# Seven products instead of eight in ten down projections of a one-core decoder layer

## Chip, core and metric

One Trainium2 chip; the kernel runs on one of its cores. The metric is the device time of one execution in microseconds. Before the change the median of three runs is 2538.48 us (2538.07 to 2540.17).

## What is computed

One layer of a hybrid decoder for 512 prompt positions and 8 single sample positions, 520 tokens in all, in float32. A first half mixes tokens (stick-breaking attention over 8 heads, with 1024 cached positions for each sample, and a chunked gating MLP), projects the result and adds it to the residual `h`. Then, with D_MODEL = 2048, D_FF = 5632 and PLE_DIM = 256:

```
f = rmsnorm(h, g_ffn)
h = h + (silu(f @ w_gate) * (f @ w_up)) @ w_down
h = h + sigmoid(rmsnorm(h, g_ple) @ w_ple_gate) * (p @ w_ple_proj)
```

The change touches the second of these lines.

## The kernel before

All activations lie transposed: 128 features on the partitions, 520 tokens in the free dimension, so `h` is 16 tiles of 128x520. The tokens are taken in two halves of 260. Every product of float32 matrices is made of three matmuls on halves rounded to a shorter format: high weight times high activation, high times low, low times high. Each weight block therefore needs a high half `w_hi` (a rounding copy on ACT, called a high below) and a low half `w_lo` (raw minus high, a subtraction on DVE, a low). A job is one such pair of operations on 1024 columns, 8 blocks of 128x128. Raw weights come from DRAM by DMAs that SP issues, one unit of 2048 columns (1024 KB) each.

The feed-forward runs over D_FF in 11 chunks of 512 features. Four blocks of features make a chunk, and they are computed in pairs: two feature blocks by 520 tokens by 2048 inputs is a 2x2 by 2x2 block product, done by seven products instead of eight (Strassen's scheme in Winograd's form). So a chunk has four pairs of tiles, two for the gate and two for the up projection, in the order g0, u0, g1, u1. Each pair (`pair_of_tiles`) has seven products of 24 matmuls of 128x260 (`product`), seven operand pairs `ops` that were built once from `f` on DVE and ACT ahead of and during the first pair, and four sums of weights on DVE (`add_weights`, into `w_sum` and in place of one raw half). Between the products ACT copies partial results from PSUM (`copy_part`) and DVE joins them (`join`); at the end of a gate pair ACT applies SiLU into `yg`, and at the end of an up pair DVE multiplies, ACT rounds `yg` into `act_hi` and DVE subtracts into `act_lo`.

The down projection of a chunk multiplies its 512 features by w_down into all 16 tiles of `h`. It is plain: `down_tiles` takes 16 tiles, for each 4 blocks x 3 terms x 2 token halves = 24 matmuls. ACT drains each finished tile from PSUM into one of four slots of `staging`, and POOL adds two slots at a time to the residual `h_dram` in DRAM by a DMA that accumulates (520 KB, `accum_op=ALU.add`). The down part of chunk c is placed behind the pair g0 of chunk c + 1, so there are ten such parts; the eleventh (`last_down`) adds straight into `h` in SBUF, reloaded from `h_dram`, and is followed by the gate of the last line of the reference, 16 tiles of 96 matmuls.

The order on every engine is written out by hand, and semaphores with counted values tie them together: `ended` counts products or tiles that PE has finished, `hi_done` and `lo_done` the jobs of ACT and DVE, `staged` the drains, `h_added` the landings of the accumulating DMAs, `w_summed` the sums of weights, `joined`, `copied`, `gate_read`, `up_read` and `silu_done` the steps at a pair's end. ACT, DVE and SP run the chunks 1 to 10 in a hardware loop (`Fori`), PE and POOL have them written out. The ring of `w_hi` and `w_lo` holds four jobs, the ring of raw weights three units (two in `w_raw`, one in `w_extra`). ACT makes the high half of the job four ahead of the product that just ended. SP's queue in the feed-forward holds only these loads, each behind a wait for a low or a sum that frees its slot, and at the end the reload of `h` in four DMAs of 1040 KB, and of `proj`.

Lines of the profile that are spoken of: L1737 mixer and output projection; L1954 plain matmuls (`plain_block`: down parts, last down part, gate, side projection); L1969 matmuls of pairs; L1041 highs; L1522 lows (L1260 those of the first half of the layer); L1535 sums; L1562 joins; L1126 drains; L1074 copied partial results; L795 accumulating DMAs; L739 loads of cached values; L790 the side projection's stores; L1615, L1620, L1627 operands of the first pair.

Of the kernel before, what the change touches and what calls it, by code (L numbers as in the profile page):

```python
# [27 lines left out]
P = 128  # L28
# [40 lines left out]
PAIR = 7  # L69
CHUNK_JOBS = 4 * PAIR + 2 * FFN_GROUP  # L70
CHUNK_ENDS = 4 * PAIR + KT
CHUNK_LOADS = 3 * FFN_GROUP
RAW_SLOTS = 3
JOB0 = 2 * U_FFN
STAGES = 4


Pair = namedtuple("Pair", "job end pair load")
Down = namedtuple("Down", "job end load")

PROJ_JOBS = 4
FIRST = [Pair(PROJ_JOBS + PAIR * i, KT + PAIR * i, i, 2 + 2 * i) for i in range(4)]


def chunk(job, end, pair, load):

    jobs, ends, loads = (PAIR, 2 * FFN_GROUP, PAIR, PAIR, PAIR), (PAIR, KT, PAIR, PAIR, PAIR), (2, 4, 2, 2, 2)
    out = []
    for i in range(5):
        if i == 1:  # L90
            out.append(Down(job, end, load))
        else:
            out.append(Pair(job, end, pair, load))
            pair += 1
        job, end, load = job + jobs[i], end + ends[i], load + loads[i]
    return out


LOOP = chunk(PROJ_JOBS + 4 * PAIR, KT + 4 * PAIR, 4, 2 + 8)
NEXT = chunk(LOOP[0].job + CHUNK_JOBS, LOOP[0].end + CHUNK_ENDS, 8, LOOP[0].load + CHUNK_LOADS)[0]  # L100
LAST_IT = FFN_CHUNKS - 2
LAST_DOWN = Down(NEXT.job + CHUNK_JOBS * LAST_IT, NEXT.end + CHUNK_ENDS * LAST_IT,
                 NEXT.load + CHUNK_LOADS * LAST_IT)
GATE_JOB = LAST_DOWN.job + 2 * FFN_GROUP
GATE_END = LAST_DOWN.end + KT
GATE_LOAD = LAST_DOWN.load + FFN_GROUP
# [84 lines left out]
def build(nc, w_units, x_t, p_t, cache_k, cache_v, page_table, g_mix, g_out, g_ffn, g_ple, g_q, g_k,  # L191
          ln_g, ln_b, w_s_t, b_s, sb_bias, w_s00, y_t, k_t, v_t, chunk_v_t):
    h_dram = nc.dram_tensor("h_dram", (P, KT, TOK), F32, kind="Internal").ap()
    proj_dram = nc.dram_tensor("proj_dram", (P, KT, TOK), F32, kind="Internal").ap()
    q_rows_dram = nc.dram_tensor("q_rows_dram", (SAMPLES, HEADS * P), F32, kind="Internal").ap()

    with ExitStack() as ctx:
# [18 lines left out]
        w_raw = sb("w_raw", [P, 2, SLOTS * P])  # L216
        w_hi = sb("w_hi", [P, 2, SLOTS * P], F32R)
# [33 lines left out]
        with ExitStack() as ffn:  # L251
            ops[6] = operand(6, ffn)
            act_hi = sb("act_hi", [P, FFN_GROUP, TOK], F32R, where=ffn)
            act_lo = sb("act_lo", [P, FFN_GROUP, TOK], F32R, where=ffn)
# [41 lines left out]
        with ExitStack() as ffn:  # L296
            staging = sb("staging", [P, STAGES, TOK], where=ffn)
            yg = sb("yg", [P, 2, TOK], where=ffn)
            part = sb("part", [P, 4, HALF], where=ffn)
            w_sum = sb("w_sum", [P, GROUPS * P], where=ffn)  # L300
            w_extra = sb("w_extra", [P, SLOTS * P], where=ffn)
# [16 lines left out]
        tok_ps = ctx.enter_context(nc.psum_tensor("tok_ps", [P, 512], F32))  # L318
        mix_ps = ctx.enter_context(nc.psum_tensor("mix_ps", [P, 512], F32))
# [14 lines left out]

        def raw(i):

            return w_extra[:, :] if i % RAW_SLOTS == 2 else w_raw[:, i % RAW_SLOTS, :]

        def landed(i, it=0):

            slot = i % RAW_SLOTS
            before = 0 if slot == 2 else U_FFN // 2
            return w_in[slot], 16 * (before + i // RAW_SLOTS + 1) + it * (16 * CHUNK_LOADS // RAW_SLOTS)

        def half_slot(w, job):

            return w[:, job % 4 // 2, job % 2 * GROUPS * P:(job % 2 + 1) * GROUPS * P]
# [10 lines left out]
        up_acc = (mix_ps[:, 0:HALF], out_ps[:, 1, 0:HALF], out_ps[:, 0, 0:HALF])  # L358
        pair = pair_ps[:, :, 0:HALF]
# [8 lines left out]
        w_in = [sem(f"w_in{i}") for i in range(RAW_SLOTS)]  # L368
# [12 lines left out]
        h_added = [sem(f"h_added{i}") for i in range(STAGES // 2)]  # L381
# [28 lines left out]
        act_hi_done = sem("act_hi_done")  # L410

# [72 lines left out]
        def _(sp):  # L484
# [52 lines left out]
            for u in range(U_FFN):  # L537
# [36 lines left out]
                if u == U_OUT_SB + 4:  # L574
                    sp.wait_ge(p_lo_done, 2)
                    sp.dma_start(raw(2), w_units[U_FFN]).then_inc(w_in[2], 16)
# [9 lines left out]
            def after_low(job, it=0):  # L586

                sp.wait_ge(lo_done, it * CHUNK_JOBS + (JOB0 + job + 1 - POOL_LO))

            def after_sums(pair, it=0):  # L590

                sp.wait_ge(w_summed, it * 16 + 4 * (pair + 1))

            def load(i, unit, it=0):

                if isinstance(it, int):
                    src = w_units[unit + it * CHUNK_UNITS]
                else:
                    src = w_units[bass.ds(it * CHUNK_UNITS + unit, 1), :, :].rearrange("a p n -> (a p) n")
                sp.dma_start(raw(i), src).then_inc(w_in[i % RAW_SLOTS], 16)  # L600

            after_low(1)
            load(3, U_FFN + 2)
            for k in range(KT - 2, KT):
                keep_h(k)
            after_low(3)
            load(4, U_FFN + 1)
            after_sums(0)
            load(5, U_FFN + 3)
            after_low(FIRST[0].job + 6)  # L610
            load(6, U_FFN + 4)
# [190 lines left out]
        def _(act):  # L802
# [408 lines left out]
            with act.Fori(0, LAST_IT) as it:  # L1211
                chunk_of_tiles(NEXT, it)
# [944 lines left out]
```

## Time and profile before

| | us |
|---|---|
| median of three runs | 2538.48 |
| the profiled execution | 2537.53 |
| its span | 2535.8 |
| PE busy, matmuls | 2492.0 |
| DVE busy | 1452.1 |
| ACT busy | 1014.6 |
| POOL busy | 235.1 |

The span is the time from the first to the last instruction that the profile holds; the execution's own time is 1.7 us more. Matmuls are pipelined: one is shown 282 ns long, but the next begins before it ends, so the pace is read from the length of a stretch and the number of matmuls in it. A row of a table by stage names the stretch in us from the span's start, its length, the busy time of each engine with the number of instructions, the granted TensorE clock as a share of full speed, the share of time in which the DMA engines were busy, and GB/s.

### The profile page before, as it was taken

How to read it: one execution, taken by the hardware profiler on the slowest of the kernel's cores; microseconds unless marked ns; L12 is line 12 of the kernel's file. 1: busy time of each engine (PE TensorE's matmuls, PEld its weight loads, DVE VectorE, ACT ScalarE, POOL GpSimd, SP SyncE). 2: the span in 40 equal slices, each digit the busy share in tenths (PEclk: the TensorE clock that was granted, in tenths of full speed). 3: DMA queues.
4: the chain of work that ended last, by engine and by line, in shares of the span. 5: the costliest groups of instructions: out<-in, count | busy, mean ns of one | idle time of the engine just before them, and what ended most of it. 6: DMA issues, size and time to landing. Idle time of an engine off the chain costs nothing.

```text
span 2535.8 us, 47986 instructions
## 1 busy us (share of the span) xinstructions
PE 2492.0 (98%) x20428; PEld 2469.4 (97%) x20428; DVE 1452.1 (57%) x1588; ACT 1014.6 (40%) x1351; POOL 235.1 (9%) x266
## 2 busy tenths in 40 slices
PE   6998999999999998999999999999999999999999
PEld 6998999999999998999999999999999999999999
DVE  6368776554446468555555555555555555557433
ACT  4333233333433364444444444444444444445221
POOL 4000111011101220000000000000000000003000
PEclk9999999999999999999999999999999999999999
DMA  4245665554432442454545454545444554445322
GB/s 184 101 159 191 242 217 215 184 192 142 161 116 101 159 152 100 138 130 140 128 141 126 142 126 142 126 142 126 142 126 142 126 143 125 143 125 201 137 98 85
DMA packets 73343, 368.58 MB, mean 145 GB/s; under 512 B 9658, under 2 KB 9658, under 8 KB 45378
## 3 DMA queue, kind: packets, MB, share of 16 engines
q1 hardware_dynamic: 50994, 285.29, 31.7%
q0 software_dynamic: 22016, 80.42, 15.0%
q8 instruction: 161, 2.64, 0.4%
q14 instruction: 28, 0.23, 0.0%
q10 hardware_dynamic: 144, 0.01, 0.0%
HBM read 305.98 MB, written 59.70 MB: 144 GB/s over the span
## 4 chain that ended last, share of the span: by engine, by line
PE 92%; DVE 6%; DMA 1%; issue 1%; ACT 0%; SPq 0%; DVEq 0%; ACTq 0%
PE out_ps L1954 27%; PE out_ps L1737 22%; PE pair_ps L1969 12%; PE mix_ps L1969 10%; PE out_ps L1969 7%; PE tok_ps L1969 5%; PE out_ps L1859 4%; PE pair_ps L1776 1%; DVE x_lo L1269 1%; DVE w_lo L1260 1%; DVE op_lo L1627 1%; DVE dot_s L1292 1%; DVE k_ring L1291 1%; PE tok_ps L1844 0%; DMA k_ring<-cache_k 0%
## 5 line engine op out<-in xcount | busy, mean ns | idle before, releaser
L1737 PE MATMUL out_ps<-x_hi,w_hi 128*128 128x260 f32 x1792 | 382.1, 295 | 20.3 <-DVE w_lo L1260 10.5
L1522 DVE TENSOR_TENSOR w_lo<-w_raw,w_hi 128x1024 fp32r<-128x1024 f32 x196 | 238.9, 1223 | 234.7 <-ACT w_hi L1041 234.7
L1737 PE MATMUL out_ps<-x_hi,w_lo 128*128 128x260 f32 x1792 | 363.7, 285 | 0.0
L1737 PE MATMUL out_ps<-x_lo,w_hi 128*128 128x260 f32 x1792 | 363.0, 284 | 0.0
L1737 PEld LDWEIGHTS out_ps<-x_hi,w_hi 128*128 128x128 f32 x1792 | 281.2, 191 | 24.8 <-DVE w_lo L1260 9.4
L1954 PE MATMUL out_ps<-act_hi,w_hi 128*128 128x260 f32 x1400 | 281.7, 282 | 0.0
L1954 PE MATMUL out_ps<-act_lo,w_hi 128*128 128x260 f32 x1400 | 280.8, 282 | 0.0
L1954 PE MATMUL out_ps<-act_hi,w_lo 128*128 128x260 f32 x1400 | 280.3, 281 | 0.0
L1737 PEld LDWEIGHTS out_ps<-x_hi,w_lo 128*128 128x128 f32 x1792 | 279.1, 190 | 0.0
L1737 PEld LDWEIGHTS out_ps<-x_lo,w_hi 128*128 128x128 f32 x1792 | 278.8, 190 | 0.0
L1041 ACT ACTIVATE w_hi<-w_raw 128x1024 fp32r<-128x1024 f32 x196 | 205.4, 1052 | 141.7 <-PE out_ps L1954 75.5
L1969 PE MATMUL pair_ps<-op_hi,w_hi 128*128 128x260 f32 x880 | 249.7, 284 | 6.7 <-issue 3.4
L1969 PE MATMUL pair_ps<-op_hi,w_lo 128*128 128x260 f32 x880 | 250.2, 284 | 0.0
L1969 PE MATMUL pair_ps<-op_lo,w_hi 128*128 128x260 f32 x880 | 249.7, 284 | 0.0
L1522 DVE TENSOR_TENSOR w_lo<-w_sum,w_hi 128x1024 fp32r<-128x1024 f32 x132 | 161.7, 1225 | 134.6 <-ACT w_hi L1041 133.4
L1954 PEld LDWEIGHTS out_ps<-act_lo,w_hi 128*128 128x128 f32 x1400 | 216.3, 188 | 0.0
L1954 PEld LDWEIGHTS out_ps<-act_hi,w_lo 128*128 128x128 f32 x1400 | 215.8, 188 | 0.0
L1954 PEld LDWEIGHTS out_ps<-act_hi,w_hi 128*128 128x128 f32 x1400 | 214.9, 188 | 0.0
L1126 ACT ACTIVATE staging<-out_ps 128x520 f32<-128x520 f32 x160 | 97.1, 607 | 285.0 <-PE out_ps L1954 285.0
L814 ACT ACTIVATE w_hi<-w_raw 128x1024 fp32r<-128x1024 f32 x116 | 116.4, 1050 | 220.6 <-PE out_ps L1737 219.6
L1969 PE MATMUL mix_ps<-op_hi,w_hi 128*128 128x260 f32 x704 | 198.7, 282 | 2.7 <-ACT part L1074 2.6
L1522 DVE TENSOR_TENSOR w_lo<-w_extra,w_hi 128x1024 fp32r<-128x1024 f32 x100 | 121.9, 1223 | 137.6 <-ACT w_hi L1041 137.6
(247 smaller groups left out, 5505.9 us busy)
## 6 DMA issues: line engine op xcount, KB each, us to landing
w_raw<-w_units SPq DMA_DIRECT2D x155, 1024.0 KB, 4.8
w_extra<-w_units SPq DMA_DIRECT2D x50, 1024.0 KB, 4.8
h_dram<-staging POOLq DMA_DIRECT2D x80, 520.0 KB, 5.6
k_ring<-cache_k SPq DMA_DIRECT2D x50, 512.0 KB, 5.1
v_ring<-cache_v POOLq DMA_DIRECT2D x43, 512.0 KB, 4.9
acc<-cache_v POOLq DMA_DIRECT2D x21, 512.0 KB, 4.8
k_third<-cache_k SPq DMA_DIRECT2D x14, 512.0 KB, 4.4
h<-x_t SPq DMA_DIRECT2D x4, 1040.0 KB, 10.5
```

The lines of the kernel that those rows point to most:

```text
L814: act.activation(w_hi[:, u % 2, cols], w_raw[:, u % 2, cols], ACT.Copy).then_inc(hi_done, 1)
L1041: act.activation(half_slot(w_hi, job), src, ACT.Copy).then_inc(hi_done, 1)
L1126: act.activation(halves(staging[:, t % STAGES, :]), tile_ps(t), ACT.Copy).then_inc(staged, 1)
L1260: dve.tensor_tensor(w_lo[:, u % 2, cols], w_raw[:, u % 2, cols], w_hi[:, u % 2, cols], ALU.subtract).then_inc(lo_done, 1)
L1269: dve.scalar_tensor_tensor(out=x_lo[:, slot, :], in0=src, scalar=gain, in1=x_hi[:, slot, :], op0=ALU.mult, op1=ALU.subtract).then_inc(x_lo ...
L1291: chained(dve.tensor_tensor(k_slot(j), k_slot(j), q_rows[:, :], ALU.mult))
L1292: dve.tensor_reduce(dot_s[:, pg * HEADS:(pg + 1) * HEADS], k_slot(j).rearrange("p (h d) -> p h d", h=HEADS), AXIS.X, ALU.add)\
L1522: dve.tensor_tensor(half_slot(w_lo, job), src, half_slot(w_hi, job), ALU.subtract)\
L1737: mm = pe.matmul(out_ps[:, 2 * (t % 2) + a, 0:HALF], w[:, u % 2, cols], x[:, a * HALF:(a + 1) * HALF], start=first and n == 0, stop=last a ...
L1859: mm = pe.matmul(o_s_ps(u)[:, hd:hd + 1], v_slot(j)[:, hd * P:(hd + 1) * P], a_s[:, b % 3, at:at + 1], start=False, stop=j == pages[-1], s ...
L1954: mm = pe.matmul(tile[:, a, :], w, x[:, a * HALF:(a + 1) * HALF], start=first and n == 0, stop=last and n == 2)
L1969: mm = pe.matmul(acc, w, x[:, g, :], start=fresh and g == 0 and n == 0, stop=g == GROUPS - 1 and n == 2, skip_group_check=True)
```

## The change

The ten down parts are computed by the same scheme of seven products. A unit of w_down (512 features by 4 tiles of outputs) is taken as 2x2 blocks of 256 by 256, the chunk's activations as 2x2 blocks of 256 features by 260 tokens. There are four units in a part, so 28 products, each of 2 x 2 blocks x 3 terms = 12 matmuls of 128x260, into 2x260 columns of PSUM. Products 3, 4 and 6 of a unit run on top of products 0, 1 and 2 in the same banks, so some of the final additions happen there; those that remain go through DRAM.

- ACT drains each of the 28 products as 2x260 columns, into six slots (four of `staging`, two made of `part`), product k behind the landing of product k - 6.
- POOL issues 28 accumulating DMAs of 260 KB a part instead of 8 of 520 KB. Four of seven add one quarter (two tiles by half the tokens, so two pieces of 1040 bytes in each partition) to `h_dram`; three go to helper arrays `q_dram`, `r11_dram`, `r22_dram` (2080 bytes in one piece), which the first part writes and the others add to. After the tenth part five accumulating DMAs inside DRAM add the helper arrays to `h_dram`, and SP waits for them before it reloads `h`.
- DVE makes four sums of 512 columns for each unit; highs and lows in a down part are 28 of 512 columns instead of 8 of 1024. The operands `b11`, `b2`, `t13`, `t24` are built from `yg` in the following gate pair: four differences and four lows on DVE, four highs on ACT. The eleventh part keeps `act_hi` and `act_lo`.
- The ring of `w_hi` and `w_lo` is six pieces of 512 columns, three jobs of a pair; the room of the fourth holds `w_sum` and a fifth slot of raw weights. Raw weights lie in five slots of 1024 columns and are loaded by halves of a unit, 512 KB each.
- The feed-forward of SP, ACT and DVE is written out, with no hardware loop, from a plan made when the program is built (`ITEMS`, `HIGHS`, `FREED`, `LOADS`). In the first pair one subtraction of the side projection's weights is placed before the last tile of the output projection, and the order of sums, lows and highs is changed.

```diff
 def add_job(size, end):
+    pos = JOB_POS[-1] + JOB_SIZE[-1] if job else 0
+    for i in range(pos, pos + size):
+        HOLDER[i] = job
+    FREED.append(JOB_END[HOLDER[pos + size - 1 - SUBS]] if job >= PROJ_JOBS - 1 else 0)
...
+DOWN_BANKS = (bank_x, bank_z, bank_v, bank_x, bank_z, bank_y, bank_v)
+DOWN_BEFORE = (None, None, None, 0, 1, None, 2)
...
 # PE
-def down_tiles(item, free, it=0):
-    for t in range(KT):
-        if t % 2 == 0:
-            after_low(item.job + t // 2, it)
-        free(t)
-        for k in range(FFN_GROUP):
-            plain_block(item.job + t // 2, t % 2 * FFN_GROUP + k, tile_ps(t), act_hi[:, k, :],
-                        act_lo[:, k, :], k == 0, k == FFN_GROUP - 1)
+def down_tiles(item):
+    pair0 = 4 * (item.n + 1)
+    pe.wait_ge(act_lo_done, lows_of_up(2 * (item.n + 1)))
+    for k in range(DOWN_JOBS):
+        u, i = divmod(k, UNIT_JOBS)
+        job = item.jobs + k
+        if k == 1:
+            pe.wait_ge(joined, 3 * pair0)
+        elif k == 2:
+            pe.wait_ge(gate_read, 2 * (item.n + 1) + 1)
+            pe.wait_ge(joined, 3 * pair0 + 1)
+        elif k == 5:
+            pe.wait_ge(joined, 3 * pair0 + 3)
+            pe.wait_ge(up_read, 2 * (item.n + 1))
+        before = [j for j in range(k) if DOWN_BANKS[j % UNIT_JOBS] is DOWN_BANKS[i]]
+        if before:
+            pe.wait_ge(staged, DOWN_JOBS * item.n + before[-1] + 1)
+        after_low(job)
+        fresh = DOWN_BEFORE[i] is None
+        for a in range(2):
+            for c in range(2):
...
+                for n, (w, x) in enumerate(((w_h, hi), (w_h, lo), (w_l, hi))):
+                    mm = pe.matmul(DOWN_BANKS[i][:, a, :], w, x, start=fresh and c == 0 and n == 0,
+                                   stop=c == 1 and n == 2, skip_group_check=True)
+        mm.then_inc(ended, 1)
...
 # ACT
+def high(job, dst, src):
+    act.wait_ge(ended, FREED[job])
+    act.activation(dst, src, ACT.Copy).then_inc(hi_done, 1)
+def down_tiles(item):
+    for k in range(DOWN_JOBS):
+        if k == STAGES:
+            act.wait_ge(joined, 3 * (4 * (item.n + 1) + 1))
+            act.wait_ge(silu_done, 2 * (item.n + 1) + 1)
+        if stage_uses(item.n, k):
+            act.wait_ge(h_added[k % DOWN_STAGES], 16 * stage_uses(item.n, k))
+        after_end(item.end + k + 1)
+        act.activation(stage(k), DOWN_BANKS[k % UNIT_JOBS], ACT.Copy).then_inc(staged, 1)
+        highs(item.end + k + 1)
...
 # POOL
-            pool.dma_start(h_dram[:, m:m + 2, :], staging[:, slot:slot + 2, :], accum_op=ALU.add)\
-                .then_inc(h_added[slot // 2], 16)
+for n in range(FFN_CHUNKS - 1):
+    extra = ALU.add if n else ALU.bypass
+    for k in range(DOWN_JOBS):
+        u, i = divmod(k, UNIT_JOBS)
+        pairs = slice(2 * u, 2 * u + 2)
+        dst, op = ((residual(u, 0, 0), ALU.add), (residual(u, 1, 1), ALU.add), (r22_dram[:, pairs, :], extra),
+                   (q_dram[:, pairs, :], extra), (residual(u, 0, 1), ALU.add),
+                   (r11_dram[:, pairs, :], extra), (residual(u, 1, 0), ALU.add))[i]
+        pool.wait_ge(staged, DOWN_JOBS * n + k + 1)
+        pool.dma_start(dst, stage(k), accum_op=op).then_inc(h_added[k % DOWN_STAGES], 16)
+for i in range(DOWN_STAGES):
+    pool.wait_ge(h_added[i], 16 * stage_uses(FFN_CHUNKS - 1, i))
+pool.dma_start(quarter(1, 1), sums_of(q_dram), accum_op=ALU.add).then_inc(merged[0], 16)
...
+pool.wait_ge(merged[0], 16 * 4)
+pool.dma_start(quarter(1, 1), sums_of(r22_dram), accum_op=ALU.add).then_inc(merged[1], 16)
...
 # DVE
+def down_sums(item, u, n):
+    h0, total = item.loads + 2 * u, as_blocks(down_sum(u))
+    if n == 0:
...
+        add_weights(total, blocks_of(h0 + 1, 0), blocks_of(h0 + 1, 1))
+        dve.wait_ge(w_summed, item.sums + 4 * u + 1)
+        add_weights(blocks_of(h0 + 1, 0), blocks_of(h0, 0), blocks_of(h0 + 1, 0), ALU.subtract)
+    elif n == 1:
+        after_low(item.jobs + UNIT_JOBS * u + 1)
+        add_weights(total, total, blocks_of(h0, 0), ALU.subtract)
+    else:
+        after_low(item.jobs + UNIT_JOBS * u + 3)
+        add_weights(total, blocks_of(h0, 1), total, ALU.subtract)
...
+def down_weights(item, after):
+    low_down(item, 6)
+    for u in range(1, 4):
+        down_sums(item, u, 0)
+        low_down(item, UNIT_JOBS * u)
+        low_down(item, UNIT_JOBS * u + 1)
+        down_sums(item, u, 1)
...
+        down_sums(item, u, 2)
+        for k in range(4, UNIT_JOBS):
+            low_down(item, UNIT_JOBS * u + k)
+    for stage in range(4):
+        begin(after, stage)
```

## Rows read from the trace of the kernel before

**Rows 1.** The page: busy time, and the chain that ended last, by engine.

```profile
PE 2492.0 (98%) x20428; PEld 2469.4 (97%) x20428; DVE 1452.1 (57%) x1588; ACT 1014.6 (40%) x1351; POOL 235.1 (9%) x266
...
PE 92%; DVE 6%; DMA 1%; issue 1%; ACT 0%; SPq 0%; DVEq 0%; ACTq 0%
```

**Rows 2.** Waits of PE from 890 us on: us in total, times, longest.

```profile
PE pair_ps L1969 <- issue: 3.4, 2, 2.0
PE pair_ps L1969 <- DVE w_lo L1522: 3.4, 1, 3.4
```

**Rows 3.** Table by stage: a down part, the four pairs beside it.

```profile
1055.90:1101.80 45.90, 45.90 (x387) 45.90 (x386) 13.29 (x11) 17.37 (x25) 6.04 (x7) 1.00 0.74 161
1101.80:1182.24 80.44, 80.44 (x674) 80.44 (x674) 58.13 (x61) 37.84 (x51) 0.85 (x1) 1.00 0.37 120
```

**Rows 4.** The chain in order of time: start, us, what.

```profile
922.20 1.14 DVE w_lo L1260
...
1055.92 45.87 PE out_ps L1954 x384
```

**Rows 5.** Timeline of DVE: start, us, what.

```profile
1037.29 0.42 DVE L1589 SCALAR_TENSOR_TENSOR yg<-mix_ps,yg 128x260 f32<-128x260 f32 x1
1037.63 0.42 DVE L1591 SCALAR_TENSOR_TENSOR yg<-part,yg 128x260 f32<-128x260 f32 x1
...
1093.08 1.22 DVE L1535 TENSOR_TENSOR w_extra<-w_raw,w_extra 128x1024 f32<-128x1024 f32 x1
1094.22 1.22 DVE L1535 TENSOR_TENSOR w_sum<-w_sum,w_raw 128x1024 f32<-128x1024 f32 x1
```

**Rows 6.** Timeline of ACT in a down part.

```profile
1061.69 0.61 ACT L1126 ACTIVATE staging<-out_ps 128x520 f32<-128x520 f32 x1 [2.26 <-PE out_ps L1954]
1062.19 1.05 ACT L1041 ACTIVATE w_hi<-w_extra 128x1024 fp32r<-128x1024 f32 x1
1064.56 0.61 ACT L1126 ACTIVATE staging<-out_ps 128x520 f32<-128x520 f32 x1 [1.31 <-PE out_ps L1954]
```

**Rows 7.** DMAs issued by POOL, by form: busy us, mean ns, idle before.

```profile
L795 POOL DMA_DIRECT2D h_dram<-staging x80 | 68.3, 854 | 1232.2 <-ACT staging L1126 1215.3 <-issue 16.9
L739 POOL DMA_DIRECT2D v_ring<-cache_v x43 | 23.5, 547 | 188.0 <-PE out_ps L1859 177.9 <-issue 10.1
...
L790 POOL DMA_DIRECT2D proj_dram<-proj_stage x16 | 8.7, 544 | 14.2 <-ACT proj_stage L1028 13.8 <-POOL h_sum L780 0.3
```

**Rows 8.** DMA, 1096.9 to 1102.7 us: busy tenths, GB/s, GpSimd's queue.

```profile
DMA  1010100000990434589599989899897712000000
GB/s 29 0 29 0 29 0 0 0 0 0 287 172 0 29 29 86 86 143 201 115 230 201 230 172 258 172 230 230 172 287 143 144 29 29 0 0 0 0 0 0
...
q0 software_dynamic: 148, 0.55, 59.5%
```

**Rows 9.** DMA, 1101.8 to 1182.24 us: the hardware queue.

```profile
q1 hardware_dynamic: 1225, 8.99, 32.1%
```

**Rows 10.** DMA, 1081.8 to 1092 us: two accumulating, one load of weights.

```profile
DMA  9469899999995779979699759989998963100000
GB/s 131 49 114 179 163 261 212 212 212 212 354 257 225 289 289 418 418 321 482 257 387 307 210 177 195 196 163 212 245 212 163 245 114 65 16 16 0 0 0 0
...
q0 software_dynamic: 269, 0.99, 55.2%
q1 hardware_dynamic: 144, 1.05, 28.5%
```

**Rows 11.** DMAs, KB, us to landing: page; last row 920.7 to 941 us.

```profile
h_dram<-staging POOLq DMA_DIRECT2D x80, 520.0 KB, 5.6
k_ring<-cache_k SPq DMA_DIRECT2D x50, 512.0 KB, 5.1
...
proj_dram<-proj_stage POOLq DMA_DIRECT2D x13, 260.0 KB, 3.5
```

**Rows 12.** Timeline of POOL: an issue that met a DVE operation.

```profile
1062.60 0.91 POOL L795 DMA_DIRECT2D h_dram<-staging  x1 [122.53 <-ACT staging L1126]
```

More of the change, by code:

```diff
@@ L68 @@
 GROUPS = KT // 2
[L69 to L73, printed above, removed]
+SUB = GROUPS * P // 2
+SUBS = 6
+RAW_SLOTS = 5
 JOB0 = 2 * U_FFN
 STAGES = 4
-Pair = namedtuple("Pair", "job end pair load")
-Down = namedtuple("Down", "job end load")
+DOWN_STAGES = 6
 PROJ_JOBS = 4
[L82 to L96, printed above, removed]
@@ L99 @@
[L99 to L106, printed above, removed]
+UNIT_JOBS = 7
+DOWN_JOBS = 4 * UNIT_JOBS
+Pair = namedtuple("Pair", "n end jobs loads sums downs")
@@ new lines, with add_job @@
+Down = namedtuple("Down", "n end jobs loads sums")
+Plain = namedtuple("Plain", "end jobs loads")
+Load = namedtuple("Load", "unit half slot turn after")
+JOB_POS, JOB_SIZE, JOB_END, FREED, LOADS = [], [], [], [], []
+HIGHS = defaultdict(list)
+HOLDER = {}
+FREE = deque([(0, "low", 0), (1, "low", 1), (2, "low", 2), (4, "out", U_OUT + 2 * KT), (3, "low", 3)])
+def add_job(size, end):
+    job = len(JOB_POS)
+    pos = JOB_POS[-1] + JOB_SIZE[-1] if job else 0
+    JOB_POS.append(pos)
+    JOB_SIZE.append(size)
+    JOB_END.append(end)
+    for i in range(pos, pos + size):
+        HOLDER[i] = job
+    FREED.append(JOB_END[HOLDER[pos + size - 1 - SUBS]] if job >= PROJ_JOBS - 1 else 0)
+    return job
@@ new lines, in add_down, with add_plain @@
+def add_down(n, end, sums, unit):
+    item = Down(n, end, len(JOB_POS), len(LOADS), sums)
+    for k in range(DOWN_JOBS):
+        HIGHS[FREED[add_job(1, end + k + 1)]].append((item, k))
+    for u in range(4):
+        for half in range(2):
+            add_load(unit + u, half)
+        for half in range(2):
+            release(item.loads + 2 * u + half, "low", item.jobs + UNIT_JOBS * u + 5 + half)
+    return item
+def add_plain(end, unit, units, ends):
+    item = Plain(end, len(JOB_POS), len(LOADS))
+    for k in range(2 * units):
+        HIGHS[FREED[add_job(2, end + ends(k))]].append((item, k))
+        add_load(unit + k // 2, k % 2)
+        release(item.loads + k, "low", item.jobs + k)
+    return item
@@ L602, in _ @@
[L602 to L611, printed above, removed]
-            after_sums(1)
-            load(7, U_FFN + 6)
-            after_low(FIRST[1].job + 6)
-            load(8, U_FFN + 5)
-            after_sums(2)
-            load(9, U_FFN + 7)
```

726 lines of the change are left out of this document (400 added, 326 removed).

## The prediction

> **What bounds the kernel now.** I read the page's busy shares and chain first. PE is busy 98% of the span and holds 92% of the chain [rows 1]. The list of who waited for whom, for PE from 890 us on, is nearly empty: 10.7 us in all, of which the two longest are in the first pair of tiles [rows 2]. From 1055.9 us the table by stage shows PE busy for the whole of each stretch at a granted clock of 1.00 [rows 3]: a down part takes 45.9 us for 384 matmuls (0.1195 us each), the four pairs beside it 80.4 us for 672 (0.1197 us). In the chain a down part is one unbroken PE piece [rows 4]. So in the feed-forward nothing but the number of matmuls counts, and every one taken away is worth 0.1195 us as long as no other engine, queue or transfer becomes slower than PE. Before that, in the first pair, the chain goes through DVE [rows 4].
>
> **What the change takes off PE.** A down part was 16 tiles x 4 blocks x 3 terms x 2 halves = 384 matmuls of 128x260. It becomes 4 units x 7 products x 4 blocks x 3 terms = 336 of the same shape, each with its own weight load as now. 48 x 0.1195 = 5.73 us a part, 57.3 us in ten. A product of a unit takes 12 x 0.1195 = 1.43 us, a part 28 x 1.43 = 40.1 us.
>
> **What DVE gets.** Two 1024-column operations start 1.14 us apart, two of 260 columns 0.34 us [rows 5]; by the line between them 512 columns cost 0.60 us. A unit needs four sums and seven subtractions of 512 columns, 11 x 0.60 = 6.6 us in its 10.0 us of PE. In a gate pair the building of the operands adds five operations of 260 columns and three of 520 (0.61 us): 3.5 us onto seven subtractions and four sums of 1.14 and three joins of 0.34, 17.1 us beside 20.1 us of PE; the subtraction of 1040 columns in each up pair goes. DVE stays below PE in both. Following the order written out, a low half in a down part is done some 1.9 us after the product six before it ended, and PE needs it 7.2 us after. With room for three jobs of 1024 columns instead of four, a pair's low half still has two products, 5.7 us, for a high half of 1.05, a low half of 1.22 and at most two sums. Zero; if this cover went, a late low half would cost PE its lateness once per product.
>
> **What ACT gets.** A drain of 520 columns and a high half of 512 start about 0.5 us apart each [rows 6]: 1.0 to 1.2 us per 1.43 us product. The tightest place is the start of a part: after the gate pair ends, ACT makes two high halves, the first behind a sum, then three SiLUs, and only then drains product 0, about 3.4 us after the pair's end, while PE wants that bank at 3 x 1.43 = 4.3 us, and the bank of the gate sum at 2.9 us against some 1.6. Both fit by 1 us. Zero, with 3 us a part as the other end (a rival).
>
> **What POOL and the DMA get.** Here the trace shows no like of what is added. Eight accumulating DMAs of 520 KB a part become 28 of 260 KB: 4.26 MB become 7.45 MB. Sixteen of them write two pieces of 1040 bytes a partition, twelve a whole 2080. POOL first. Issuing took 0.854 us for the accumulating 128 rows, 0.544 us for a plain 128 rows, whether of 2080 or of 4096 bytes [rows 7]; so it goes by rows and kind, not by bytes. For 256 pieces the nearest bounds are 0.85 (pieces free) and 1.71 us (twice). I take the upper end: 12 x 0.86 + 16 x 1.71 = 37.7 us in 40.1.
> Then the engines. In a stretch with one accumulating DMA alone, the digits of the busy row add up to 16.3 slices of 0.145 us, 2.36 us, and as digits are cut down, up to 2.6; take 2.5 us for 520 KB, 1.25 us for 260 KB, and this is what the 215 GB/s of its full slices gives too [rows 8]. The queue's own share counts overlapping packets twice and is the upper bound: 59.5% of 5.8 us = 3.45 us, 1.73 us for 260 KB. The lower bound is the plain rate, 0.7 us. Weights run at the same time: the hardware queue took 32.1% of 80.44 us for 8.99 MB [rows 9], so 1.50 us for a 512 KB half unit, eight in a part, 12.0 us. Together 28 x 1.25 + 12.0 = 47.0 us of work in a part of 40.1 us. Where both kinds ran together now, 0.99 and 1.05 MB were done in 7.2 us of busy engines (the digits give 26.8 slices of 0.255 us, 6.8 us, plus half of what they cut off) against 4.7 + 3.0 = 7.7 one after the other [rows 10], so about 45 us. Some of this may run late. Drain k waits only for the landing of k - 6, 6 x 1.43 - 0.6 = 8.0 us after it was staged; landing took 5.6 us for 520 KB [rows 11], so 4.3 to 5.2 us for 260 KB (half the movement, up to twice the issue), which leaves about 3.3 us; and PE returns to a bank after three products at the earliest, 2.3 us after a prompt drain, less what ACT is busy with, 1.7 us. Cover: 5 us a part. 45 - 5 = 40 to 47.0 - 5 = 42.0 us: a stall of 0 to 1.9 us a part. I take 1.0, so 10 us in ten, with 0 and 15.3 us a part (28 x 1.73 + 12.0 - 5 - 40.1) as ends.
> A rule of the Trainium skill speaks against such transfers: "DMA: Bandwidth & Descriptors", "Anatomy of one DMA", gives each one from GpSimd about 2.0 us and its bytes over 436 GB/s, an estimate of 2.6 us here and 73 us for 28 if nothing overlaps. The sum would then be about 2537.5 + 10 x (73 - 45.9) = 2809 us. The thirteen plain DMAs of 260 KB that landed 3.5 us after issue within 20.3 us [rows 11] overlap, so the fixed part is latency here; as a rival it has rival 5.
>
> **The rest.** Weight halves of 512 KB land in 5.1 us [rows 11]; in the order of loads the tightest one has 4.5 us before DVE's sum and that sum 3 us of its own. Zero. The first pair: one 1024-column subtraction moves ahead of DVE's chain into its idle time, -1.1 us [rows 4, 5]; the loads it needs are out before. The join at the end: five accumulating DMAs inside DRAM with 1024 pieces each, by 0.854 us per 128 about 6.8 us to issue, 34 us, plus two landings of some 8 us: 50 us in the 54.6 us between the tenth part's end and the moment SP loads the residual again. Zero, up to 10 us once if the pieces cost more. Loops written out on ACT, DVE and SP: PE shows no gap at them, zero. The last down part and the gate keep their matmuls; half the gate's weights of a tile can be prepared only one tile ahead, 5.7 us for about 3.7 us of work. Zero.
>
> **Sum.** From the profiled execution, 2537.5 us (its span of 2535.8 and 1.7 around it): -57.3 -1.1 +10 = 2489.1. The median of the runs is 1.0 us above the profiled one: 2490 us.
>
> **Rivals.**
> 1. The accumulating queue becomes the bound: slower. Place: drains on ACT waiting for landings, and PE waiting for drains, in the ten down parts. At 1.73 us a transfer a part takes 28 x 1.73 + 12.0 - 5 = 55.4 us against 45.9 before: +9.5 x 10, 2633 us. It decides from 1.38 us a transfer, where a part is as long as before. For it: 74% of the engines' time is busy in a down part already [rows 3], and both the bytes and the number of pieces grow. Against: the peaks of 290 GB/s for accumulation alone and over 450 GB/s with weights beside it [rows 8, 10]. 15%.
> 2. The same, only between: 1.32 to 1.38 us a transfer. At 1.35 a part takes 44.8 us, 4.7 us over PE: 2527 us. 12%.
> 3. POOL's issuing is the bound. It needs over 2.17 us for 256 pieces ((40.1 + 5 - 10.3)/16). If each of them also waited for one of DVE's 0.60 us operations, 1.71 + 0.60 = 2.31: a part of 42.3 us, +22, 2502 us. One issue that met a DVE operation took 0.91 instead of 0.85 us [rows 12], which speaks against it. 8%. The Trainium skill, "SBUF — State Buffer", "SBUF: two separate sides", says that DVE keeps GpSimd off a shared port pair in two-port modes, or with two SBUF sources if the GpSimd operation reads SBUF; the row agrees that writing descriptors beside such sums is hardly held up.
> 4. The change doesn't deliver its 5.7 us: ACT's queue at the start and end of each part is late by 3 us, 30 us in all, 2510 us. For it: the margins of 1 us above. Against: before, ACT idles more than a microsecond ahead of each drain [rows 6]. 10%.
>
> 5. The transfers don't overlap at all: a landing of 4.3 us each, 28 x 4.3 = 120 us a part, 3280 us. Against it the overlap in [rows 11]; 1%, and taken out of the 15% of rival 1. The rule of "DMA: Bandwidth & Descriptors" above is its milder form.
>
> **Chances and range.** The forecast (a stall of 0 to 2 us a part, 2479 to 2500) has 55%. Noise is about 0.2%, 5 us. Faster: 55 + 10 + 8 and most of the second rival, 80%; within 0.2%, 5%; slower, 15%. The range goes from 2476 (no stall at all and a better start) to 2540; what it leaves out is rival 1 and little else.
>
> **What would show it.** Down parts of 336 matmuls and 40 to 42 us, pairs still 80.4 us; DMA busy 0.9 or more in a down part; ACT's drains waiting for landings late in a part, by less than 1 us each. POOL issues of 1.7 us for the split rows and 0.86 for the others. It is wrong if parts are 45 us or longer (rivals 1 and 2: waits for landings; rival 3: POOL never idle in a part), if pairs grow beyond 81 us (the shorter rings), or if the last down part begins late behind the reload of the residual.

## The result and the profile after

The changed kernel takes 2572.65 us (median of 4 runs, 2568.15 to 2580.49) against 2538.28 us before (2537.31 to 2540.17). The ratio is 1.0138, 95% interval 1.0110 to 1.0166: it is slower by 1.4%, and the forecast of 2490 us and its range of 2476 to 2540 were wrong. The profiled execution took 2575.6 us (span 2574.0) beside 2537.5 before.

The page of the changed kernel: busy time, the accumulating queue, the chain by engine.

```profile
PE 2468.4 (96%) x19948; PEld 2439.2 (95%) x19948; DVE 1692.9 (66%) x2088; ACT 1170.9 (45%) x1731; POOL 473.3 (18%) x471
...
q0 software_dynamic: 75728, 117.71, 23.1%
...
PE 64%; DMA 16%; DVE 12%; ACT 4%; issue 3%; POOL 1%; SPq 0%; DVEq 0%; ACTq 0%; POOLq 0%
...
h_dram<-staging POOLq DMA_DIRECT2D x130, 260.0 KB, 9.8
```

The 480 matmuls are gone, but PE's share of the chain fell from 92% [rows 1] to 64%, and transfers hold 16%. A landing takes 9.8 us for 260 KB, where it took 5.6 us for 520 KB [rows 11]. The list of PE's waits, nearly empty in this part of the kernel before [rows 2], has three new entries (us in total, times, longest):

```profile
PE tok_mix L2118 <- ACT staging L1240: 27.5, 10, 4.1
PE pair_ps L2181 <- ACT staging L1240: 26.1, 19, 2.1
...
PE out_ps L2102 <- DVE h L1859: 8.4, 1, 8.4
```

And behind ACT's drains stand the landings; the list of waits of ACT:

```profile
ACT staging L1240 <- DMA h_dram<-staging: 96.1, 93, 3.7
```

L2181 is a product of a down part, L1240 its drain, L2118 a pair of tiles. In nearly every one of the ten parts PE waits twice for a bank whose drain waits for a slot of the ring, and once more, mostly longest, at the first product of the next pair. The table by stage shows one period: the pairs, the down part with its waits, and what follows.

```profile
1746.07:1829.90 83.83, 83.83 (x687) 83.83 (x688) 66.99 (x83) 40.26 (x60) 2.11 (x2) 0.98 0.41 118
1829.90:1875.81 45.91, 39.45 (x323) 38.86 (x322) 28.61 (x41) 30.66 (x55) 27.97 (x26) 1.00 1.08 225
1875.80:1881.00 5.20, 5.19 (x30) 5.20 (x31) 2.21 (x2) 2.01 (x4) 2.11 (x2) 0.67 1.16 215
```

The period is 129.7 us, from one such wait's end to the next, against 126.3 before [rows 3]. In the part's stretch 6.5 us are idle on PE, the DMA share is 1.08, and POOL, the engine that issues the 28 transfers, is busy for 28.0 of 45.9 us. A DMA share above 1 is possible because the view adds up packets that overlap. The third row is the surprise: behind the wait the granted clock is 0.67 over 5.2 us. PE's timeline shows it in the starts of its matmuls: 0.12 us apart at first, 0.22 us apart from 1876.77 to 1879.8, then 0.12 again.

```profile
1875.81 0.36 PE L2118 MATMUL tok_mix<-op_hi,w_hi 128*128 128x260 f32 x1 [3.44 <-ACT staging L1240]
...
1876.48 0.29 PE L2118 MATMUL tok_mix<-op_hi,w_lo 128*128 128x260 f32 x1
1876.60 0.37 PE L2118 MATMUL tok_mix<-op_hi,w_hi 128*128 128x260 f32 x1
1876.77 0.42 PE L2118 MATMUL tok_mix<-op_lo,w_hi 128*128 128x260 f32 x1
1876.99 0.42 PE L2118 MATMUL tok_mix<-op_hi,w_lo 128*128 128x260 f32 x1
...
1879.81 0.40 PE L2118 MATMUL tok_mix<-op_hi,w_hi 128*128 128x260 f32 x1
```

That is the lower level of 1.2 GHz for about 3 us. The product takes 4.63 us instead of 2.87, so the stall costs 1.76 us more than its own 3.4. The same happens at eight of the ten pair starts, and not only behind the long waits. Two of the starts with a short wait, from the timeline, and their products, from the chain:

```profile
1746.07 0.36 PE L2118 MATMUL tok_mix<-op_hi,w_hi 128*128 128x260 f32 x1 [1.91 <-ACT staging L1240]
2265.87 0.36 PE L2118 MATMUL tok_mix<-op_hi,w_hi 128*128 128x260 f32 x1 [1.87 <-ACT staging L1240]
```

```profile
1746.07 4.65 PE tok_mix L2118 x24
2265.87 3.13 PE tok_mix L2118 x24
```

The first of them is slow, the second isn't. In the three parts that end with such a short wait, 24 matmuls behind the wait before it, inside the part, were slow too (4.2 to 4.5 us instead of 3.0, behind waits of 1.72, 1.75 and 2.13 us), while other waits of 1.71 and 1.74 us had no such effect. So the length of one wait alone doesn't tell whether the clock falls.

The chain of waits goes along the ring (start, us, what):

```profile
1841.66 10.48 DMA h_dram<-staging
1852.14 0.02 issue
1852.16 0.61 ACT staging L1240
1852.77 0.29 issue
1853.06 1.20 POOL h_dram L870
1854.26 0.16 issue
1854.42 9.78 DMA h_dram<-staging
...
1865.13 9.78 DMA h_dram<-staging
1874.90 0.02 issue
1874.92 0.61 ACT staging L1240
1875.54 0.28 issue
1875.81 4.63 PE tok_mix L2118 x24
```

A slot comes round in 10.7 us (1854.42 to 1865.13), about 9.8 of them a landing. Six slots give one transfer per 1.785 us, and a product takes 1.43 us. The DMA view of this stretch (busy tenths, GB/s, queues):

```profile
DMA  0289599999999999999999999999999999999999
GB/s 14 43 246 198 90 262 250 187 212 204 193 197 224 335 316 322 241 200 198 205 203 195 205 222 308 322 324 259 208 191 204 197 198 202 247 327 320 326 216 194
...
q0 software_dynamic: 5034, 6.07, 82.3%
q1 hardware_dynamic: 1152, 4.19, 25.8%
```

From the sixth slice on the engines are full. The movement is near 200 GB/s where accumulation is alone and 310 to 330 where a weight load runs beside it. Between 1850 and 1856 us almost nothing but accumulation runs; the queue's line for these 6 us, and the one for the whole period from 1746.07 to 1875.81 us:

```profile
q0 software_dynamic: 938, 1.20, 118.6%
```

```profile
q0 software_dynamic: 6092, 7.47, 35.4%
```

So 260 KB take 1.33 us of full engines (1.20 MB in 6 us, 200 GB/s). By the queue's share, which counts overlapping packets twice and therefore passes 100%, it is 0.354 x 129.74 / 28 = 1.64 us each. The stretch of the part alone can't be divided by 28: only 6.07 MB, 22.8 transfers' worth, moved in it, and the last ones land behind it.

### The profile page after: what moved, and what is told of

Read it like the earlier page. It is cut to its first block, busy times and chain, and to the rows that moved or that the text cites. A ratio compares the mean times of both kernels' runs of the same rounds, so it can differ in the third digit from the quotient of the medians.

```text
span 2574.0 us, 47687 instructions
## 1 busy us (share of the span) xinstructions
PE 2468.4 (96%) x19948; PEld 2439.2 (95%) x19948; DVE 1692.9 (66%) x2088; ACT 1170.9 (45%) x1731; POOL 473.3 (18%) x471
## 3 DMA queue, kind: packets, MB, share of 16 engines
q0 software_dynamic: 75728, 117.71, 23.1%
## 4 chain that ended last, share of the span: by engine, by line
PE 64%; DMA 16%; DVE 12%; ACT 4%; issue 3%; POOL 1%; SPq 0%; DVEq 0%; ACTq 0%; POOLq 0%
PE out_ps L1885 22%; DMA h_dram<-staging 14%; PE tok_mix L2118 12%; PE out_ps L2102 9%; PE pair_ps L2118 7%; PE out_ps L2118 6%; PE out_ps L2007 4%; DVE w_lo L1613 3%; DVE w_sum L1625 2%; ACT w_hi L1132 1%; ACT staging L1240 1%; PE pair_ps L1924 1%; POOL h_dram L870 1%; DMA k_ring<-cache_k 1%; DVE x_lo L1358 1%
## 5 line engine op out<-in xcount | busy, mean ns | idle before, releaser
L1613 DVE TENSOR_TENSOR w_lo<-w_sum,w_hi 128x1024 fp32r<-128x1024 f32 (+1 forms) x252 | 244.7, 971 | 179.1 <-ACT w_hi L1132 176.7
L1132 ACT ACTIVATE w_hi<-w_raw 128x1024 fp32r<-128x1024 f32 (+1 forms) x306 | 264.2, 866 | 159.2 <-PE out_ps L2102 103.1
L2118 PE MATMUL tok_mix<-op_hi,w_hi 128*128 128x260 f32 x1056 | 303.7, 288 | 29.0 <-ACT staging L1240 27.5
L1132 ACT ACTIVATE w_hi<-w_sum 128x1024 fp32r<-128x1024 f32 (+1 forms) x252 | 214.8, 852 | 204.4 <-DVE w_sum L1625 152.2
L2118 PE MATMUL tok_mix<-op_hi,w_lo 128*128 128x260 f32 x1056 | 304.0, 288 | 0.0
L2118 PE MATMUL tok_mix<-op_lo,w_hi 128*128 128x260 f32 x1056 | 303.2, 287 | 0.0
L2118 PE MATMUL pair_ps<-op_hi,w_hi 128*128 128x260 f32 x880 | 249.5, 283 | 8.7 <-DVE op_lo L1793 5.0
L2118 PE MATMUL pair_ps<-op_hi,w_lo 128*128 128x260 f32 x880 | 249.8, 284 | 0.0
L2118 PE MATMUL pair_ps<-op_lo,w_hi 128*128 128x260 f32 x880 | 249.4, 283 | 0.0
L2118 PEld LDWEIGHTS tok_mix<-op_hi,w_hi 128*128 128x128 f32 x1056 | 204.4, 194 | 31.0 <-issue 29.3
L905 ACT ACTIVATE w_hi<-w_raw 128x1024 fp32r<-128x1024 f32 x115 | 115.3, 1049 | 221.4 <-PE out_ps L1885 220.3
L2118 PEld LDWEIGHTS tok_mix<-op_hi,w_lo 128*128 128x128 f32 x1056 | 204.3, 194 | 0.0
L2118 PEld LDWEIGHTS tok_mix<-op_lo,w_hi 128*128 128x128 f32 x1056 | 204.2, 193 | 0.0
L2118 PEld LDWEIGHTS pair_ps<-op_hi,w_hi 128*128 128x128 f32 x880 | 166.8, 190 | 9.4 <-issue 7.5
```

Source lines behind the costliest of these rows:

```text
L905: act.activation(w_hi[:, u % 2, cols], w_raw[:, u % 2, cols], ACT.Copy).then_inc(hi_done, 1)
L1132: act.activation(dst, src, ACT.Copy).then_inc(hi_done, 1)
L1613: dve.tensor_tensor(slot(w_lo, job), src, slot(w_hi, job), ALU.subtract).then_inc(lo_done, 1)
L2118: mm = pe.matmul(acc, w, x[:, g, :], start=fresh and g == 0 and n == 0, stop=g == GROUPS - 1 and n == 2, skip_group_check=True)
```

## Experiments

Each ratio is against runs of the kernel before taken beside it: 2537.12 us for e1, e2, e3 and e5, 2537.64 us for e4, e6, e7 and e8, 2537.37 us for e9, e10 and e11.

**e1: the same transfers, nothing added.**

```diff
-                    pool.dma_start(dst, stage(k), accum_op=op).then_inc(...)
+                    pool.dma_start(dst, stage(k), accum_op=ALU.bypass).then_inc(...)
```

> The changed kernel with all 28 DMAs of a down part as plain writes, so the residual and the helper arrays hold only the last part's products: the addition is left out, all else stays. Theory (the accumulating transfers fill the DMA engines in the down parts, some 1.33 us for 260 KB, and ACT's drains wait for landings): a plain 260 KB takes 0.7 us, 28 x 0.7 + 12 = 32 us of work in 41 us, so the 6.4 us of waits and the 1.6 us of low clock behind them go from each part: about 2495 us, 8 us of which are the late weights at the end. Rival (POOL's issuing or ACT's order are what is late): no more than 10 us better, about 2562. Rival (PE's own pace in the down part is the loss, 0.1226 us a matmul): parts without waits and the pace stays, which would leave 10 us of the loss.

Measured: 2494.44 us, ratio 0.9831 (0.9814 to 0.9847). The page, and behind it two rows of the chain, the starts of a pair five periods apart:

```profile
q0 software_dynamic: 38096, 117.71, 13.7%
...
h_dram<-staging POOLq DMA_DIRECT2D x130, 260.0 KB, 4.7
```

```profile
1580.14 2.88 PE tok_mix L2118 x24
```

```profile
2185.81 2.88 PE tok_mix L2118 x24
```

From 1190 to 2150 us PE waits for nothing. The queue moves the same bytes and lands in 4.7 us instead of 9.8. The period is (2185.81 - 1580.14) / 5 = 121.1 us. So 78 us of the changed kernel's time are the price of adding instead of writing. This also measures the gain by itself: 5.2 us a period, not 5.7. The total met the expected 2495 us partly by luck: 8 us of it were to come from the late weights at the end, and PE still waits there for 6.8 us instead of 8.4.

**e3: the kernel before, its accumulating transfers issued twice.**

```diff
+                    pool.dma_start(spare_dram[:, m:m + 2, :], staging[:, slot:slot + 2, :],
+                                   accum_op=ALU.add).then_inc(h_added[slot // 2], 16)
```

> The kernel before (plain down parts, 384 matmuls) with each accumulating DMA of 520 KB issued twice, the second into a spare array: 8.5 MB a part in pieces as before. Theory (bytes of accumulation fill the engines at about 200 GB/s beside the weights): 16 x 2.6 + 12 = 54 us of work in a part of 45.9 us with two pairs of slots to run late: parts of 48 to 52 us, 2560 to 2600 us, without any product of the new scheme. Rival (it is the latency of each transfer against a ring of six slots of 1.43 us): here a slot has 11.5 us for two transfers of 5.6 us, no wait: 2538 to 2542 us.

Measured: 2590.63 us, ratio 1.0205 (1.0188 to 1.0222), as expected: such traffic alone, with no Strassen product in a down part, slows the kernel before too. The waits count both landings. ACT's longest wait in the down parts is for them:

```profile
ACT staging L1129 <- DMA spare_dram<-staging: 202.5, 53, 6.6
```

**e2: no 1040-byte pieces.** The residual in DRAM is laid out by quarters, so that each transfer writes whole 2080-byte rows.

```diff
-    h_dram = nc.dram_tensor("h_dram", (P, KT, TOK), ...)
+    h_dram = nc.dram_tensor("h_dram", (P, 4, 2, 2, 2, HALF), ...)
```

> The changed kernel with the residual kept in DRAM as quarters (two tiles by half the tokens in one row of 2080 bytes a partition), so no transfer of a down part has pieces of 1040 bytes; the stores and the reload of the residual carry the pieces instead. Theory (bytes fill the engines): POOL's issues fall from 1.2 to 0.9 us, the rate stays near 200 GB/s, less than 3 us a part: 2545 to 2572 us. Rival (the pieces are what is slow): the 16 split transfers of a part lose 0.2 us or more each, the waits of 6.4 us a part go below 3 and the clock stays up: 2520 us or less.

Measured: 2556.34 us, ratio 1.0069 (1.0050 to 1.0088), inside the theory's window and far above the rival's 2520. The issue of a split transfer falls from 1.24 to 0.87 us and the landing from 9.8 to 9.0: 16 us less than the changed kernel, a fifth of the 78. The stores and the reload of `h` change with the layout (16 loads of 260 KB for four of 1040); PE's wait at the last down part stays near what it was, 7.8 us.

**e5: each down part cut into two halves**, with a pair of tiles between them, so that 14 transfers come at a time.

```diff
-            if c and i == 0:
-                items.append(add_down(c - 1, end, sums, unit + 8))
...
+            if c and i < 2:
+                items.append(add_down(c - 1, end, sums, unit + 8 + 2 * i, PART_JOBS * i))
...
```

> The changed kernel with each down part cut in two: units 0 and 1 behind the first gate pair of the next chunk, units 2 and 3 behind its first up pair, so a pair of 20 us lies between them; same matmuls, transfers, sums. Theory (the engines' throughput over a part of 41 us is what is short): 14 x 1.33 + 6 = 25 us of work in 20.5 us, of which 5 us may run late, and the pair behind it takes up the rest: waits below 1 us a half, no low clock: about 2495 us. Rival (latency of a transfer against the ring of six slots): the waits come from the seventh drain on in each half, 8 of 14 drains a half wait: 2540 us or more.

Measured: 2597.77 us, ratio 1.0246 (1.0229 to 1.0263). My theory was wrong here: this is slower than the changed kernel. PE's waits:

```profile
PE tok_mix L2146 <- ACT staging L1258: 32.2, 15, 3.5
PE out_ps L2130 <- DVE h L1887: 22.9, 2, 12.3
```

The chain shows landings of 9.5 to 10.7 us in these short halves too, and the pair behind a first half still waits 2.9 to 3.5 us for the last drains, with the lower clock behind it. So it isn't the mean load of the period that counts, but the rate inside a burst: a ring of six slots fills within six products. But the cut isn't a clean test of that. Waits for drains fell from 53.6 to 34.1 us in all, and some 20 us of new waits for copied partial results and low halves took their place, so that a period is 129.7 us as in the changed kernel. The 25 us by which this kernel is slower come for the most part from the end: in the chain the merge's landings (27.9 and 9.6 us) now stand ahead of the reload, the waits at the last down part are 22.9 us instead of 8.4, and the granted clock is 0.93 from 2250 to 2450 us.

**e4: proj's load moved behind four weight loads** at the last down part.

```diff
-            sp.dma_start(proj[:, 0:HEADS, :], ...)
             for i in range(LAST_DOWN.loads + 3, GATE.loads + 2 * KT):
                 load(i)
+                if i == LAST_DOWN.loads + 6:
+                    sp.dma_start(proj[:, 0:HEADS, :], ...)
```

> The changed kernel with one load moved: the 2 MB of proj that the first gate needs goes out behind the first four weight halves of the gate's ring instead of ahead of them. Theory (at the last down part the raw weights stand behind the reload of h and proj, and PE waits 8.4 us once for an h add that waits for a split): about 8 us less than the changed kernel, 2562 to 2567. Rival (the h adds wait for the reload of h itself, the weights are hidden): 2570 to 2575, no change.

Measured: 2567.84 us (2562.58 to 2569.92), ratio 1.0113 (1.0097 to 1.0130). It is 4.8 us less than the changed kernel, between the windows of theory and rival; but the ranges of the two kernels overlap, and of the 6.6 us between their profiled executions 5.1 are there by some 920 us, ahead of everything that the edit touches. What the traces show is the wait for the h add: it falls from 8.4 to 4.7 us, so the order of the loads is some half of that wait.

**e6: five slots instead of six.**

```diff
-DOWN_STAGES = 6
+DOWN_STAGES = 5
```

> The changed kernel with five staging slots instead of six for the down parts. Theory A (the part is bound by how many bytes a microsecond the DMA engines get through with accumulating writes and weights together; six slots only stand in a queue, 10.7 us a slot's cycle is six times 1.785): fewer slots in flight, each lands sooner, time unchanged, 2570 to 2580. Theory B (each accumulating transfer has a latency of about 9.8 us that doesn't depend on what else is in flight, and the ring is too short for it): the cycle stays 10.7 us, 2.14 us a transfer instead of 1.785, +0.355 x 28 = 10 us a part, 2660 to 2680. In between (latency partly queueing): about 2600.

Measured: 2606.34 us, ratio 1.0265 (1.0248 to 1.0283), +34 us, the case in between. The median landing falls from 9.8 to 8.0 us, which is close to what a queue with five instead of six in it would give, and yet the kernel is slower. Lower clock is part of it: the first product of a pair takes up to 5.5 us instead of 4.6. So a landing is for a good part queueing behind the other slots, and a latency remains that five slots cover less well; how the 34 us divide isn't shown, and no run has more than six slots. ACT's waits for it (96.1 us in the changed kernel):

```profile
ACT staging L1240 <- DMA h_dram<-staging: 153.0, 111, 4.5
```

**e8: half of each addition left out.**

```diff
+                    tiles = slice(0, 2 if op is ALU.bypass else 1)
-                    pool.dma_start(dst, stage(k), accum_op=op).then_inc(...)
+                    pool.dma_start(dst[:, tiles, :], stage(k)[:, tiles, :], accum_op=op).then_inc(...)
```

> The changed kernel with every accumulating transfer cut to its first tile (130 KB instead of 260 KB); the second tile isn't added. Number of transfers, waits and slots as they are. Theory A (bytes set the time of accumulation): 28 x 0.68 + 12 = 31 us in a part of 40, no waits for staging, 2495 to 2502. Rival (a fixed time per transfer, or the issue on POOL, sets it): 2555 to 2575.

Measured: 2492.29 us, ratio 0.9829 (0.9811 to 0.9846), 3 us below theory A's window and far from the rival's. With the number of transfers and the waits kept, half the bytes land in 5.8 us and all the waits for drains in the parts go. So the number of transfers doesn't set the price. The pieces of a split transfer are halved with the bytes (128 instead of 256, issued in 0.87 instead of 1.24 us), so this run alone doesn't tell bytes from pieces; e2, with the bytes kept and the pieces halved, gained 16 of the 78 us, which leaves most to the bytes that are added.

**e7: helper arrays written plainly, added later.** In eight of ten parts the twelve transfers to the helper arrays write fresh arrays. Twelve accumulations inside DRAM add them during the next pairs, whose DMA share is 0.41. It has e2's layout and e4's order too.

```diff
+                late = 0 < n < FFN_CHUNKS - 2
+                to_q, to_r11, to_r22 = (q_new, r11_new, r22_new) if late else (q_dram, r11_dram, r22_dram)
...
+                    for total, new in ((r22_dram, r22_new), (q_dram, q_new), (r11_dram, r11_new)):
+                        for i in range(0, HEADS, 2):
+                            pool.dma_start(total[:, i:i + 2, :], new[:, i:i + 2, :], accum_op=ALU.add).then_inc(...)
```

> h kept in DRAM by quarters (no 1040-byte pieces), proj's load moved as in the tail run, and in eight of the ten down parts the twelve transfers to the helper arrays are plain writes into fresh arrays, which are added to the running ones by twelve DRAM to DRAM accumulations during the next pairs of tiles. Theory (only accumulating transfers inside the down part are too dear; 16 x 1.36 + 12 x about 0.5 + 12 of weights = 40 us in a part of 40 us; the pairs' 80 us have room for 12 accumulations): the waits for staging nearly vanish in eight parts, 2490 to 2505, below both kernels. Rival (the accumulations disturb the pairs' weights, or the remaining sixteen still land in over 8 us): 2520 to 2550.

Measured: 2507.88 us (2497.80 to 2509.88), ratio 0.9871 (0.9847 to 0.9896), 3 us over the theory's window and below both kernels. PE's waits for drains, 53.6 us together in the changed kernel, are now

```profile
PE pair_ps L2196 <- ACT staging L1255: 3.5, 4, 1.3
PE tok_mix L2133 <- ACT staging L1255: 3.4, 2, 2.8
```

of which 5.0 us are in the tenth part, which isn't deferred. That part shows the old picture, the clock included:

```profile
2198.00:2204.00 6.00, 3.21 (x23) 3.04 (x22) 3.50 (x3) 3.18 (x5) 2.19 (x4) 0.89 1.11 262
2204.00:2210.00 6.00, 6.00 (x44) 6.00 (x44) 3.11 (x3) 2.37 (x5) 0.68 (x1) 0.83 1.09 243
```

**e11: the same kernel once more.**

> The deferred kernel once more, unchanged, for a narrower interval: 2500 to 2510.

Measured: 2507.81 us, ratio 0.9886 (0.9871 to 0.9900). This is the version to keep: 1.1% to 1.3% below the kernel before, 2.5% below the changed one.

**e9: the deferral alone**, on the changed kernel.

> The changed kernel with one thing altered: in eight of the ten down parts the twelve helper transfers are plain writes into fresh arrays, added to the running ones during the next pairs of tiles. h stays in its old layout (1040-byte pieces), proj's load where it was. Theory (sixteen accumulations instead of twenty-eight in a part are what counts, the layout was worth 16 us only because the ring was full): 2505 to 2525. Rival (the small pieces cost the same 1.6 us a part whatever else is in flight): 2507.88 + 16 + 5 = 2529 or more.

Measured: 2526.24 us (2517.76 to 2530.16), ratio 0.9950 (0.9935 to 0.9964), 1 us over the theory's window. Deferral takes 46 us off the changed kernel by itself. The time lies between the windows of theory and rival (2525 and 2529), and the runs scatter more than that, so it doesn't decide what the pieces cost when the ring is less full. The remaining 18 us to e7 are near the 16 and 5 that layout and load order were worth with a full ring. In the traces PE waits 18.9 us for drains here and 7.4 in e7, and 7.9 and 2.7 us at the last down part, together 16.7 of the 18.

**e10: e7 with the later additions left out.**

> The deferred kernel without the twelve DRAM to DRAM accumulations during the pairs: the fresh arrays are written and never added. Theory (plain writes in the part are nearly free, the accumulations in the pairs delay some weights by a few us in all): 2495 to 2503. Rival (they cost nothing, what is left of the distance to the run without any addition, 2494.44, is in the parts): 2505 to 2510.

Measured: 2501.44 us (2494.04 to 2503.42), ratio 0.9863 (0.9848 to 0.9877). About 6 us are the price of the additions beside the pairs, as the theory had it: e11, taken beside it, is 6.4 us slower and the two ranges don't meet, though e7's overlaps this one.

## Why the prediction was wrong, step by step

**PE.** The mechanism was right, the size a little off: -5.2 us a part by e1's period, -52 us instead of -57.3. In e1 a product of a down part takes 1.44 to 1.46 us instead of 1.43, without any wait; 28 of them are about 0.5 us. Why isn't settled.

**First pair.** From the output projection's last matmul to the first down part it was 143.2 us before, 140.7 to 140.8 in the changed kernel, e1 and e8, 142.4 in e4: -0.8 to -2.5 us instead of -1.1.

**DVE and ACT.** Zero was right: with plain writes (e1) PE waits for neither from 1190 to 2150 us, so the margin of 1 us held and rival 4 falls.

**POOL.** A split row's transfer was issued in 1.2 us, not 1.71, a whole one in 0.9 to 1.0. POOL idles 18 us in a part. Rival 3 falls, but the issue time is part of a slot's cycle, and by e2 the pieces cost 16 us, in issue and landing together.

**The DMA: the step that failed.** I forecast a stall of 1.0 us a part; against e1 a period grew by 129.7 - 121.1 = 8.6 us. Two terms failed. The price: I took 1.25 us a transfer and 47.0 us of work in a part of 40.1, and full engines took 1.33 us, so 28 x 1.33 + 12.0 = 49.2 us. That alone is 2.2 us a part. (The 45 us beside it should read 47.0 x 7.2 / 7.7 = 43.9; the low end of the stall is zero either way.) The cover: with 1.33 us in it, the same sum gives 0.9 to 4.1 us of stall, and PE's waits came to 5.4 us a part, so the 5 us that were to run late were not there in full. They hung on "4.3 to 5.2 us for 260 KB" for a landing, worked out from a landing in a part with two transfers in flight, by halving the movement. With six in flight, on engines that are full, it is 9.8 us: nothing of the 3.3 us of slack was left, and each slot was late by 10.7 - 6 x 1.43 = 2.1 us. A landing time read at low load isn't a latency that can be carried into a full ring. e1 (4.7 us), e8 (5.8), e6 (8.0), e2 (9.0) and the changed kernel (9.8) are landings of such transfers under different loads.

**Missed altogether: the clock after a stall.** Behind the waits come stretches at 1.2 GHz: eight of the ten pair starts take some 1.75 us longer, and three products inside the parts 1.2 to 1.6, together some 18 us. The sum had no term for what a stall costs besides itself.

**Missed: what stands at the end.** Of the merge of the helper arrays I had the parts wrong: four of its five DMAs are issued within 8 us, but they land in 17 and 21 us instead of 8, and the first goes out only at 2277.3 us, 11 us after the tenth part, when the last transfers have landed. So the reload of h started at 2322.9 us, 3.6 us ahead of the last down part instead of 5.8 before. The weights issued from 2326.9 us on stand behind it and behind `proj`. The last down part shows the wait in the chain:

```profile
2332.22 5.76 PE out_ps L2102 x48
2337.98 5.40 issue
2343.38 1.06 ACT w_hi L1132
2344.44 0.02 issue
2344.47 1.23 DVE w_lo L1613
2345.69 0.62 DVE h L1859
```

I had priced the merge at zero and up to 10 us, and named the late beginning of this part only as a sign. e1, without any stall in the ten parts, is 42.7 us below the kernel before although its parts save 52: 9 us are lost outside them. The same wait at the last down part is 6.8 of these, and the lower clock behind it some 2 (366 matmuls in 46.0 us instead of 43.8). e4 gives half of the wait to the order of the loads; what the late merge costs by itself no run shows.

**The sum again.** -52 (PE, ten parts), +9 (outside them, the first pair included), +78 (stalls and clock, the changed kernel's median less e1's) = +35, against +34.4 measured between the medians. It has to close, since the 9 and the 78 are themselves differences of medians; the forecast had -57.3, -1.1 and +10 in their places. Of the 78, PE's waits for drains are 53.6 and the clock some 18; the remaining 6 aren't assigned. Medians carry a few us of chance here: the profiled execution lost 3.8 us to the lower clock at some 260 us (16 matmuls in 3.21 us instead of 1.88), in the first half, which the change leaves alone.

**Rivals.** Rival 1 was the right mechanism, at the place it named, with ACT's drains waiting for landings. Its 1.73 us is the queue's share, and by that measure a transfer took 1.64: a part of 28 x 1.64 + 12.0 - 5 = 52.9 us, some 2606 us. By the rate of full engines, 1.33 us, it was rival 2, some 2527 us. The measured time lies between, so neither price with its cover gives it. Rival 2 falls short by 45 us since it too took 5 us of cover for granted and had nothing for the clock. "The peaks of 290 GB/s" that spoke against rival 1 were single slices of 0.145 us; the sustained rate is 200.

**The fixed time of a transfer.** The 2.0 us of the Trainium skill, "DMA: Bandwidth & Descriptors", "Anatomy of one DMA", which I set aside as latency that overlaps, does overlap: a transfer goes through every 1.785 us, less than the fixed 2.0 us alone. But a landing bounds a ring with few slots, as e6 shows. Its bandwidth, 436 GB/s, accumulation here didn't sustain: the view above shows 200 alone and 330 with weights.

## What to carry to other kernels

Before a ring of staging slots takes more traffic, work out slots x time per transfer against the landing time at the new load, not the old one; where the engines come to be full, a landing may double, and its excess falls on PE. Count an accumulating write to DRAM at twice a plain one or more (by the queue's share 1.64 us here against 0.72 in e1), and if some of its targets aren't needed soon, write them plainly and add them where the engines idle. Look behind every stall of PE for time at the lower clock: in the changed kernel all six waits of 3.4 to 4.1 us were followed by it, and two of three waits of 1.9 us.

## What the runs showed of the hardware that was not expected

- The same 117.7 MB on GpSimd's queue took 23.1% of the DMA engines' time when the down parts' share of them was added (changed kernel) and 13.7% when it was written (e1), with landings of 9.8 and 4.7 us, and the packets doubled (75728 against 38096).
- An accumulating 260 KB is issued on POOL in 1.24 us with 256 pieces and 0.87 us with 128; the plain write of 256 pieces takes 0.72 us, of 128 pieces 0.55 to 0.58 us (e1).
- After a wait of 3.44 us PE ran about 1 us at full pace and then some 3 us with matmuls 0.22 us apart, a granted clock of 0.67 over the 5.2 us. The same came after waits of 1.90 and 1.91 us, and not after one of 1.87; in e2, of nine waits of 2.6 to 2.7 us at a pair's start, six were followed by it.
- Accumulation within DRAM lands slowly: 1040 KB in 18.9 to 22.1 us in the merge (e4), 260 KB in 11.8 to 12.2 us with twelve in flight (e7).
